# A two-trunk attention and mixture kernel: one tile of u is scaled on ScalarE before the router's exponentials instead of after them

## Chip, cores and metric

The kernel runs on one core of a Trainium2 chip. The metric is the device time of one execution in microseconds (us), lower is better. The kernel before takes 1629.51 us, the median of three executions (1629.05 to 1630.3).

## What is computed

Two independent sequences of 512 tokens with 1024 features ("trunks" 0 and 1) go through one attention layer and one expert-choice mixture of 16 experts, in float32:

```python
u = rmsnorm(h, norm_mix_g)
h = h + neighbourhood_attention(u, na_w_qkv, na_rpb, na_w_o)
u = rmsnorm(h, norm_ffn_g)
# expert_choice_ffn(u):
aff = softmax(u @ router_w, axis=-1)              # 512 x 16
gate, idx = lax.top_k(aff.T, 64)                  # each expert picks 64 tokens
xs = u[idx]
hid = silu(xs @ w_gate) * (xs @ w_up)
out = (hid @ w_down) * gate[..., None]
h = h + zeros.at[idx].add(out)
return rmsnorm(h, final_norm_g)
```

## The kernel before

Tokens lie on the 128 partitions, four tiles of 128 tokens for a trunk. The attention of trunk 0 runs first, then that of trunk 1, then a loop over the 16 experts, which handle the chosen rows of both trunks together (128 rows, 64 of each trunk). Each matrix product is made of three (high by high, high by rest, rest by high), so ScalarE casts each pair of weight rows to its high part and VectorE (DVE) subtracts to get the rest; the expert loop is a long stream of such casts, subtractions and matmuls at line 1293.

Every engine's program is written out by hand and runs in that order; the engines meet only at semaphores. The place that the change touches is the end of trunk 1's attention, where the mixture begins. There:

- TensorE (PE) makes the router's logits, `logits(b, 3)` at L1568, which count in `rt_used`. DVE computes `rstd`, one over the root mean square of h, in five small steps that end at L911 (`rstd_done`).
- DVE scales the logits and subtracts their maximum (L1186 to L1190, in `lg`). ScalarE takes the exponential in `exp_logits` (L655), and DVE turns it into affinities in `aff` (L1192 sum, L1194 reciprocal, L1196 product of `lg` and the reciprocal, both in SBUF).
- PE transposes `aff` (`turn_lists(1)`, L1501), in the middle of `early_gate_up`, matmuls of expert 0 on trunk 0's rows (L1525, L1526) that stand before and behind it in PE's order. DVE then picks the 64 best tokens of each expert in a linked chain of some forty instructions (L1112 to L1125, L1131), PE transposes the tables (`turn_tables(1)`, L1507), and DVE writes the addresses of expert 0's rows of trunk 1 in `first_rows_at` (L1145, semaphore `first_done`).
- Meanwhile ScalarE's `scale_h` (L651) multiplies each of the four tiles of h (`xh`) by its `rstd` into `arena`, and counts in `scaled`. GpSimd (POOL) waits for each, multiplies it in place by the norm's weights `grow` (L514, two inputs in SBUF), and after every second tile sends two tiles to `u_rows` in HBM (L518).
- POOL's `gather(0)` (L523) waits for all of `u_rows` and for `first_done`, and reads expert 0's 64 rows of trunk 1 back into `xh`. It has this in front of it:

```python
pool.wait_ge(u_out, 32 * TRUNKS)
pool.wait_ge(h_out, 16 * TRUNKS)
pool.wait_ge(first_done, 1)
gather(0)
```

- PE, behind `turn_tables(1)`, runs 36 transposes of the identity (L1665) whose result nobody reads, and then `first_rows` (L1620), which waits for the gathered rows. The weight loads of the next steps wait for the matmuls that follow (`pair_used`, SP's queue, L450).

ScalarE's functions come from tables; a change of table is an instruction of its own (ACT_TABLE_LOAD), and `preload_act_table` places one by hand. The copies with a scale run under any of the tables used here.

Of the kernel before, what the change touches and what calls it, by code (L numbers as in the profile page):

```python
# [21 lines left out]
ACT = mybir.ActivationFunctionType  # L22
# [19 lines left out]
TILES = T // P  # L42
# [82 lines left out]
def encoder_kernel(nc, x, g_mix, g_ffn_col, g_ffn, g_fin, w_qkv, bias, w_o, router_w, w_gate, w_up, w_down, identity, y):  # L125
# [5 lines left out]
    with ExitStack() as ctx:  # L131
# [91 lines left out]
        def bank(b, n=1):  # L223
            return ps[:, b * BANK:(b + n) * BANK]
# [332 lines left out]
        def _(act):  # L557
# [12 lines left out]
            def root(c):  # L570
                act.wait_ge(var_done, c + 2)
                cols = slice(TILES * c, TILES * (c + 1) if c < 3 * TRUNKS else TILES * c + 1)
                nc.scalar.activation(sdev[:, cols], var[:, cols], ACT.Sqrt).then_inc(sdev_done, 1)
# [31 lines left out]
            def next_high(b, g, what, last_job, q):  # L605

                wait_full(act, b, g, last_job)
                high(q, SLOT["pre" if g is None else stage_name(g)][what])

            def x_squares(b, i):  # L610

                act.wait_ge(xe_in[b][i], 16)
                if i:
                    act.wait_ge(ssq_xa, 2 * b + 1)
                square(b, early_t, i, arena[:, 0, :], ssq_xa)

            def split_x(b):
                for kc in range(KC):
                    act.wait_ge(xt_front, KC * b + kc + 1)
                    k = NORM_BANKS[kc % 4] if b else FIRST_BANKS[kc]  # L620
                    nc.scalar.activation(ut_high[:, kc * T:(kc + 1) * T], bank(k), ACT.Copy,  # L621
                                         scale=g_col[:, kc:kc + 1]).then_inc(uth_done, 1)

            def before_groups(b):
                copy_q(b, None, 0)
                copy_q(b, None, 1)
                next_high(b, None, "q", "q1", SLOTS * b + 1)

            def h_squares(b, i):

                wait_copied(act, b, GROUPS - 1, f"o{2 * i}")
                wait_copied(act, b, GROUPS - 1, f"o{2 * i + 1}")
                if i:
                    act.wait_ge(ssq_h, TILES * b + i)
                square(TRUNKS + b, xh, i, squares_junk, ssq_h)

            def copy_h(b, i):
                act.wait_ge(rt_mm, 2 * (TILES * b + i) + 1)
                nc.scalar.copy(rt[i % 2][:, 0:BANK], bank(ROUTER_BANKS[i % 2])).then_inc(rt_act, 1)

            def copy_part(b, i):
                act.wait_ge(part_mm, TILES * b + i + 1)
                nc.scalar.copy(part_lg[:, :], bank(4)[:, PART_AT:PART_AT + P]).then_inc(part_done, 1)

            def scale_h(b):

                act.wait_ge(rstd_done, b + 1)
                act.wait_ge(rt_used, TILES * (b + 1))
                for i in range(TILES):
                    at = TILES * (TRUNKS + b) + i  # L650
                    nc.scalar.activation(arena[:, i, :], xh[:, i, :], ACT.Copy, scale=rstd[:, at:at + 1]).then_inc(scaled, 1)  # L651

            def exp_logits(b):
                act.wait_ge(lg_step, 3 * (b + 1))
                nc.scalar.activation(lg[:, :, :], lg[:, :, :], ACT.Exp).then_inc(lexp_done, 1)  # L655
# [63 lines left out]
            for b in range(TRUNKS):  # L719
                group(b, 0)  # L720
                with act.Fori(1, GROUPS - 1) as g:
                    group(b, g)
                group(b, GROUPS - 1)
                if b + 1 < TRUNKS:
                    x_squares(b + 1, 0)
                    x_squares(b + 1, 2)
                copy_h(b, 0)
                if b + 1 < TRUNKS:
                    root(b + 1)
                h_squares(b, 0)  # L730
                for i in range(1, TILES - 1):
                    copy_part(b, i - 1)
                    copy_h(b, i)
                    h_squares(b, i)
                    if i == 1 and b + 1 == TRUNKS:
                        act.wait_ge(early_mm, 1)
                        nc.scalar.copy(early_xt, bank(EARLY_BANK)).then_inc(early_xt_done, 1)
                nc.scalar.preload_act_table(ACT.Sqrt)
                copy_h(b, TILES - 1)
                copy_part(b, TILES - 2)  # L740
                h_squares(b, TILES - 1)
                root(TRUNKS + b)
                copy_part(b, TILES - 1)
                if b + 1 == TRUNKS:
                    exp_logits(b)
                    scale_h(b)
                if b + 1 < TRUNKS:
                    split_x(b + 1)
                if b + 1 < TRUNKS:
                    next_high(b, GROUPS - 1, "o", "o7", SLOTS * (b + 1))  # L750
                if b + 1 < TRUNKS:
                    exp_logits(b)
                    scale_h(b)
                    before_groups(b + 1)
# [532 lines left out]
        def _(pe):  # L1287
# [322 lines left out]
            for kc in range(1, KC):  # L1610
                _, last = early_gate_up(kc)
# [135 lines left out]
```

## Time and profile before

| | |
|---|---|
| median of three executions | 1629.51 us |
| the profiled execution's own time | 1629.97 us |
| its span in the profile | 1628.2 us |
| PE busy | 98% |
| DVE busy | 78% |
| ScalarE (ACT) busy | 64% |
| POOL busy | 7% |
| chain that ended last, share on PE | 94% |

The time of an execution holds 1.77 us around the span. Attention takes the first 500 us or so, the expert loop nearly all the rest. The busy shares are averages over both; the change lies in the few microseconds in between, and there the rows in time below have to be read.

### The profile page before, as it was taken

The numbers are of one execution on the slowest core, as the hardware profiler recorded it, in microseconds if no ns is written. First come the engines' busy times: TensorE is split into PE (matmuls) and PEld (weight loads), VectorE is DVE, ScalarE is ACT, GpSimd is POOL, SyncE is SP. The second block draws the span as 40 slices with busy tenths as digits, with TensorE's granted clock in tenths as the row PEclk, the third lists the DMA queues.
The fourth block names the chain that finished last, engine by engine and source line by source line (L and its number), as shares of the span: only waits on it lengthen the run. The fifth ranks groups of instructions, "written<-read, shape, count | busy, mean of one in ns | idle before, by whom it ended". The sixth has DMA issues, their size and how long they took to land.

```text
span 1628.2 us, 22708 instructions
## 1 busy us (share of the span) xinstructions
PE 1591.7 (98%) x8288; PEld 1306.3 (80%) x8288; DVE 1264.1 (78%) x1318; ACT 1034.3 (64%) x942; POOL 110.2 (7%) x60
## 2 busy tenths in 40 slices
PE   6999999999999899999999999999999999999996
PEld 5888787888785588888888888888888888888884
DVE  6564576674565588888888888888888888888887
ACT  4443356443234577777777777777777777777774
POOL 0000002000003001001010010100101001010000
PEclk9999999999999999999999999999999999999998
DMA  9333244533243999999999999999999999999997
GB/s 362 130 109 124 74 156 176 177 113 120 78 139 124 372 405 385 387 394 367 394 391 383 397 366 395 386 384 395 367 397 384 388 396 366 393 385 388 396 349 299
DMA packets 150375, 496.15 MB, mean 305 GB/s; under 512 B 9536, under 2 KB 34240, under 8 KB 150336
## 3 DMA queue, kind: packets, MB, share of 16 engines
q1 hardware_dynamic: 140224, 459.44, 74.2%
q0 software_dynamic: 8832, 33.03, 6.4%
q10 hardware_dynamic: 1280, 3.15, 0.7%
q8 instruction: 25, 0.41, 0.1%
q14 instruction: 14, 0.11, 0.0%
HBM read 471.47 MB, written 20.97 MB: 302 GB/s over the span
## 4 chain that ended last, share of the span: by engine, by line
PE 94%; DVE 2%; DMA 2%; ACT 1%; POOL 1%; issue 0%; SPq 0%; POOLq 0%; DVEq 0%; ACTq 0%
PE ps L1293 84%; PE ps L1404 2%; PE ps L1367 2%; PE ps L1376 2%; PE ps L1661 2%; PE ps L1630 1%; DMA raw<-w_up 1%; POOL arena L514 1%; PE ps L1699 0%; DMA g_col<-g_mix 0%; DMA u_rows<-arena 0%; PE ps L1589 0%; DVE w_rest L857 0%; ACT ut_high L621 0%; PE ps L1548 0%
## 5 line engine op out<-in xcount | busy, mean ns | idle before, releaser
L857 DVE TENSOR_TENSOR w_rest<-raw,w_high 128x2048 fp32r<-128x2048 f32 x220 | 501.0, 2290 | 107.0 <-ACT w_high L795 75.3
L795 ACT CAST w_high<-raw 128x2048 fp32r<-128x2048 f32 x188 | 360.1, 1915 | 146.9 <-PE ps L1293 135.1
L1293 PE MATMUL ps<-w_high,xt_high 128*128 128x512 f32 x1000 | 311.3, 392 | 0.0
L1293 PE MATMUL ps<-w_rest,xt_high 128*128 128x512 f32 x1000 | 308.4, 390 | 0.0
L1293 PE MATMUL ps<-w_high,xt_rest 128*128 128x512 f32 x1000 | 308.3, 390 | 0.0
L857 DVE TENSOR_TENSOR w_rest<-raw_more,w_high 128x2048 fp32r<-128x2048 f32 x94 | 214.0, 2289 | 43.1 <-ACT w_high L795 43.1
L857 DVE TENSOR_TENSOR w_rest<-early,w_high 128x2048 fp32r<-128x2048 f32 x92 | 209.3, 2289 | 20.7 <-ACT w_high L795 19.3
L795 ACT CAST w_high<-raw_more 128x2048 fp32r<-128x2048 f32 x94 | 180.2, 1917 | 63.8 <-PE ps L1293 62.6
L1293 PEld LDWEIGHTS ps<-w_rest,xt_high 128*128 128x128 f32 x1000 | 188.0, 188 | 39.3
L1293 PEld LDWEIGHTS ps<-w_high,xt_rest 128*128 128x128 f32 x1000 | 188.0, 188 | 39.1
L1293 PEld LDWEIGHTS ps<-w_high,xt_high 128*128 128x128 f32 x1000 | 185.9, 188 | 36.6
L795 ACT CAST w_high<-early 128x2048 fp32r<-128x2048 f32 x92 | 176.3, 1917 | 59.8 <-PE ps L1293 59.8
L1293 PE MATMUL ps<-w_high,ht_high 128*128 128x512 f32 x496 | 154.2, 392 | 0.0
L1293 PE MATMUL ps<-w_high,ht_rest 128*128 128x512 f32 x496 | 152.8, 389 | 0.0
L1293 PE MATMUL ps<-w_rest,ht_high 128*128 128x512 f32 x496 | 152.8, 389 | 0.0
L578 ACT ACTIVATE arena<-arena,nmx 128x256 f32<-128x256 f32 x128 | 63.6, 498 | 92.9 <-DVE nmx L930 92.9
L1293 PEld LDWEIGHTS ps<-w_rest,ht_high 128*128 128x128 f32 x496 | 93.1, 188 | 19.5
L1293 PEld LDWEIGHTS ps<-w_high,ht_rest 128*128 128x128 f32 x496 | 93.1, 188 | 19.4
L1293 PEld LDWEIGHTS ps<-w_high,ht_high 128*128 128x128 f32 x496 | 91.9, 188 | 18.0
L1293 PE MATMUL ps<-ut_high,w_high 128*128 128x512 f32 x256 | 102.4, 400 | 2.5 <-DVE w_rest L857 1.3
L545 POOL DMA_INDIRECT h_rows<-xh,rows x15 | 37.6, 2504 | 965.0 <-ACT xh L784 965.0
L1293 PE MATMUL ps<-ut_rest,w_high 128*128 128x512 f32 x256 | 99.8, 390 | 0.0
(203 smaller groups left out, 2006.5 us busy)
## 6 DMA issues: line engine op xcount, KB each, us to landing
raw<-w_gate SPq DMA_DIRECT2D x64, 1024.0 KB, 7.9
raw<-w_up SPq DMA_DIRECT2D x64, 1024.0 KB, 8.5
raw<-w_down SPq DMA_DIRECT2D x64, 1024.0 KB, 7.6
raw_more<-w_gate SPq DMA_DIRECT2D x32, 1024.0 KB, 9.2
raw_more<-w_up SPq DMA_DIRECT2D x32, 1024.0 KB, 10.0
early<-w_gate SPq DMA_DIRECT2D x32, 1024.0 KB, 8.7
early<-w_up SPq DMA_DIRECT2D x32, 1024.0 KB, 9.5
raw_more<-w_down SPq DMA_DIRECT2D x32, 1024.0 KB, 8.5
```

The source lines that it names most:

```text
L514: nc.gpsimd.tensor_tensor(arena[:, i, :], arena[:, i, :], grow[:, :], ALU.mult).then_inc(xs_done, 1)
L545: pool.indirect_dma_start(h_dram, bass.IndirectOffsetOnAxis(ap=rows[:, e:e + 1], axis=0), ys, None, compute_op=ALU.add).then_inc(scattered ...
L578: nc.scalar.activation(scores[hh % 2][:, i, :], scores[hh % 2][:, i, :], ACT.Exp, bias=nmx[:, hh % 2, i:i + 1], accum_out=psum_row[:, hh % ...
L795: nc.scalar.copy(w_high[:, i % SLOTS, :], raws[i % RAW_SLOTS]).then_inc(high_done, 1)
L857: nc.vector.tensor_tensor(w_rest[:, j, :], raws[j if r is None else r], w_high[:, j, :].bitcast(F32), ALU.subtract).then_inc(rest_done, 1)
L1293: done = nc.tensor.matmul(out, lhs, rhs, start=start and part == 0, stop=stop and part == 2)
L1367: last = nc.tensor.matmul(ps[:, 6 * BANK + at:6 * BANK + at + WIN], qt[on, p, tile * P:(tile + 1) * P], kt[on, p, lo:lo + WIN], start=True ...
L1376: last = nc.tensor.transpose(ps[:, at:at + P], scores[hh % 2][:, i, c * P:(c + 1) * P], ident[:, :])
L1404: last = nc.tensor.matmul(bank(4)[a * HD:(a + 1) * HD, tile * P:(tile + 1) * P], vals, pt[:, at:at + P], start=c == 0, stop=c == 1)
L1630: last = nc.tensor.transpose(bank(6, 2)[:, kc * P:(kc + 1) * P], xg[:, kc * P:(kc + 1) * P], ident[:, :])
L1661: last = nc.tensor.transpose(bank(6, 2)[:, c * P:(c + 1) * P], hid[:, c * P:(c + 1) * P], ident[:, :])
```

## The change

For trunk 1 only, ScalarE loads the table of the exponential by itself, scales the first tile of h, takes the exponentials, and then scales the other three tiles. Before, the table load stood with the exponentials, and all four tiles behind them. Trunk 0's order stays.

```diff
-            def scale_h(b):
+            def scale_h(b, lo=0, hi=TILES):
 
                 act.wait_ge(rstd_done, b + 1)
                 act.wait_ge(rt_used, TILES * (b + 1))
-                for i in range(TILES):
+                for i in range(lo, hi):
                     at = TILES * (TRUNKS + b) + i
                     nc.scalar.activation(arena[:, i, :], xh[:, i, :], ACT.Copy, scale=rstd[:, at:at + 1]).then_inc(scaled, 1)
...
                 if b + 1 == TRUNKS:
+                    nc.scalar.preload_act_table(ACT.Exp)
+                    scale_h(b, 0, 1)
                     exp_logits(b)
-                    scale_h(b)
+                    scale_h(b, 1, TILES)
```

ScalarE's order at the end of trunk 1's attention before, with the semaphores that each instruction waits for (`gv` holds part of the logits here, L643 copies them for PE):

```order
L573 ACTIVATE sdev<-var 128x4 [waits var_done]
L643 COPY gv<-ps 128x128 [waits part_mm]
L655 ACT_TABLE_LOAD
L655 ACTIVATE lg<-lg 128x64 [waits lg_step]
L651 ACTIVATE arena<-xh,rstd 128x1024 [waits rt_used,rstd_done]
L651 ACTIVATE arena<-xh,rstd 128x1024 x3
```

And the same place of the changed kernel:

```order
L573 ACTIVATE sdev<-var 128x4 [waits var_done]
L643 COPY gv<-ps 128x128 [waits part_mm]
L745 ACT_TABLE_LOAD
L651 ACTIVATE arena<-xh,rstd 128x1024 [waits rt_used,rstd_done]
L655 ACTIVATE lg<-lg 128x64 [waits lg_step]
L651 ACTIVATE arena<-xh,rstd 128x1024 [waits rt_used,rstd_done]
L651 ACTIVATE arena<-xh,rstd 128x1024 x2
```

One scaled tile moved in front of the exponential; the table load is still one and stands where it stood. The other engines' programs are the same, line numbers apart.

## Rows read from the trace of the kernel before

**Rows 1.** The page, part 4: the chain that ended last, by line
```profile
PE ps L1293 84%; PE ps L1404 2%; PE ps L1367 2%; PE ps L1376 2%; PE ps L1661 2%; PE ps L1630 1%; DMA raw<-w_up 1%; POOL arena L514 1%; PE ps L1699 0%; DMA g_col<-g_mix 0%; DMA u_rows<-arena 0%; PE ps L1589 0%; DVE w_rest L857 0%; ACT ut_high L621 0%; PE ps L1548 0%
```

**Rows 2.** Windows: stretch, length, busy (count) of PE, PEld, DVE, ACT, POOL, PE clock, DMA
```profile
560.00:1590.00 1030.00, 1030.00 (x4728) 857.09 (x4727) 909.07 (x440) 777.77 (x455) 77.69 (x30) 1.00 1.01 386
```

**Rows 3.** The chain in order of time, 495 to 580: start, us, what
```profile
505.53 4.70 POOL arena L514 x2
...
511.29 4.70 POOL arena L514 x2
...
516.28 6.06 DMA u_rows<-arena
...
522.61 3.64 DMA xh<-u_rows,first_rows_at
...
531.29 10.17 DMA raw<-w_up
```

**Rows 4.** Timeline of ScalarE: start, us, operation [idle before <-releaser]
```profile
501.93 0.25 ACT L643 COPY gv<-ps 128x128 f32<-128x128 f32 x1
502.20 1.28 ACT L655 ACT_TABLE_LOAD   x1
504.08 0.26 ACT L655 ACTIVATE lg<-lg 128x64 f32<-128x64 f32 x1 [0.60 <-DVE lg L1190]
504.24 4.25 ACT L651 ACTIVATE arena<-xh,rstd 128x1024 f32<-128x1024 f32 x4
```

**Rows 5.** Timeline of DVE at the same place
```profile
502.87 0.16 DVE L911 TENSOR_TENSOR rstd<-newt 128x4 f32<-128x4 f32 x1
...
503.82 0.23 DVE L1190 TENSOR_TENSOR lg<-lg,lstat 128x64 f32<-128x64 f32 x1
504.37 0.22 DVE L1192 TENSOR_REDUCE lstat<-lg 128x4 f32<-128x64 f32 x1 [0.32 <-ACT lg L655]
...
504.84 0.29 DVE L1196 TENSOR_TENSOR aff<-lg,lstat 128x128 f32<-128x128 f32 x1
...
521.24 0.15 DVE L1145 SCALAR_TENSOR_TENSOR first_rows_at<-topt 64x1 uint32<-64x1 f32 x1
```

**Rows 6.** Timeline of PE at the same place
```profile
502.23 0.39 PE L1568 MATMUL ps<-adder,gv 128*128 128x16 f32 x2 [0.52 <-ACT gv L643]
...
505.19 0.63 PE L1501 MATMUL ps<-ident,aff 128*64 128x128 f32 x4 [0.69 <-DVE aff L1196]
...
519.93 0.27 PE L1507 MATMUL ps<-ident,gv 64*128 64x64 f32 x1 [1.95 <-DVE gi L1131]
...
520.20 5.82 PE L1665 MATMUL ps<-ident 128*128 128x128 f32 x36
526.29 0.70 PE L1620 MATMUL ps<-ident,xh 64*128 64x64 f32 x8 [0.28 <-DMA xh<-u_rows,first_rows_at]
```

**Rows 7.** Windows of L1665 alone: stretch, length, PE (count), PEld (count), PE clock, DMA
```profile
521.00:523.00 2.00, 2.00 (x11) 2.00 (x10) 0.50 0.78 213
524.50:525.50 1.00, 1.00 (x11) 1.00 (x10) 1.00 0.56 209
```

**Rows 8.** Timeline of POOL, the first multiply alone
```profile
505.53 2.37 POOL L514 TENSOR_TENSOR arena<-arena,grow 128x1024 f32<-128x1024 f32 x1 [4.66 <-ACT arena L651]
```

**Rows 9.** All issues of gathers at L525: ns min/median/max, first and last start
```profile
L525 POOL DMA_INDIRECT xh<-u_rows,rows x15: 990/2780/2795, 527.8 to 1506.8; - x15
```

**Rows 10.** Timeline of POOL in the expert loop
```profile
623.36 2.76 POOL L525 DMA_INDIRECT xh<-u_rows,rows  x1 [0.30 <-issue]
```

**Rows 11.** Timeline of DVE beside it
```profile
622.97 2.29 DVE L857 TENSOR_TENSOR w_rest<-raw_more,w_high 128x2048 fp32r<-128x2048 f32 x1 [1.40 <-ACT w_high L795]
```

**Rows 12.** Timeline of POOL near the end
```profile
1582.35 1.19 POOL L549 DMA_INDIRECT v<-h_rows,rows  x1 [7.87 <-DMA h_rows<-xh,rows]
```

**Rows 13.** Timeline of DVE beside it
```profile
1580.39 4.48 DVE L857 TENSOR_TENSOR w_rest<-early,w_high 128x2048 fp32r<-128x2048 f32 x2
```

## Prediction

> **What bounds the kernel now.** I read first the chain that ended last. It is matmuls of the expert loop for 84% of the span [rows 1], and from 560 to 1590 us TensorE is busy for the whole of 1030.00 us [rows 2]. Nothing in the change touches that loop. Its start is what can move: a shift of the first product of the mixture is carried to the end by an engine that never waits after it.
>
> So I read the same chain in order of time around 500 us, where attention hands over to the mixture [rows 3]. It goes through POOL's multiply of u by the norm's weights (two and two tiles, 4.70 us each pair), the second store to HBM (6.06 us, landed at 516.28 + 6.06 = 522.34), the gather of expert 0's rows (3.64 us, landed at 522.61 + 3.64 = 526.25), PE's transposes of these rows at 526.29 [rows 6], some matmuls, and a load of weights of 10.17 us that those release. POOL could begin at 505.53 because ScalarE began tile 0 at 504.24 [rows 4], 1.29 us before.
>
> Two other chains run beside it with little to spare, and the timelines show them. The list of chosen tokens: exponential, affinities, choice, and `first_rows_at` at 521.24 + 0.15 = 521.39 [rows 5], for which the gather waits too; it is 522.34 - 521.39 = 0.95 us early. And PE's own order: behind the tables' transposes at 519.93 stand 36 spare transposes that end at 520.20 + 5.82 = 526.02 [rows 6], only 0.27 us before the gathered rows are used.
>
> **The change, step by step.**
>
> *Scaling tile 0.* It needs the table (502.20 + 1.28 = 503.48), rstd (502.87 + 0.16 = 503.03) and the last logits (502.23 + 0.39 = 502.62) [rows 4 to 6]. So it begins at 503.50 in place of 504.24: 0.74 us earlier, in time in which ScalarE only waited for `lg` (0.60 us idle). POOL's first multiply, 1.29 us behind, begins at 504.79. The table load itself neither moves nor is added.
>
> *The exponential.* Four scaled tiles take 4.25 us, the last 1.13 of which is one tile by itself (an estimate from the chain's share of the first, 505.38 - 504.24), so tiles follow each other at 1.04 us. The exponential begins at 503.50 + 1.04 = 504.54 in place of 504.08: 0.46 us later. The sum at L1192, 504.37 before, moves to 504.83, and the product at L1196, 504.84 before, is due at 505.30. Tiles 1 to 3 follow from 504.70 on, in time for POOL's 2.35 us a tile.
>
> *If nothing else happened*, u would land in HBM 0.74 us earlier, at 521.60. But `first_rows_at` is then 0.46 later, at 521.85. With the 0.15 us that POOL needs from a producer's end to its start (505.38 to 505.53), the gather begins at 522.0 and lands at 525.65, 0.60 earlier. PE, however, is held 0.46 us longer at L1501, everything behind it shifts by as much, and its spare transposes end at 526.48. Their end depends on the clock: at the granted clock 0.50 some 0.21 us each, at 1.00 some 0.11 (eleven overlapping in 2.00 us and in 1.00 us) [rows 7]. At 1.00 throughout, the 36 would take about 35 x 0.11 + 0.27 = 4.1 us, 1.7 less than the 5.82 here, and end at 524.8. So the first product moves by +0.2 us (spare transposes last, the clock as in this trace) or by -0.6 us (gather last, full clock).
>
> *What POOL and DVE do to each other.* Before, DVE's last operation with both inputs in SBUF, L1196, ended at 504.84 + 0.29 = 505.13, and POOL's multiply began at 505.53: they never met [rows 5, 8]. Afterwards the multiply runs from 504.79 to 507.15 (2.37 us), and L1196 is due in the middle of it, at 505.30. The trace never shows such a pair, but it shows a related one. A gather's issue on POOL takes 990 ns at best, in the first gather, when DVE had little to do, and 2780 ns in the median, inside the expert loop [rows 9]. The one at 623.36 ended at 626.12, 0.86 us after the end (625.26) of a DVE subtraction of two SBUF inputs that had begun before it [rows 10, 11]: as though POOL had stood still until DVE was through. Against it: the gather's issue at 1582.35 took 1.19 us although DVE was in a pair of such subtractions until 1584.87 [rows 12, 13]. I take the exclusion as real and mutual, that the later one stands still until the earlier one ends. The least this costs is nothing (they overlap freely), the most the rest of the two multiplies that POOL issues back to back (to 504.79 + 4.70 = 509.49).
>
> The Trainium skill, SBUF — State Buffer, section "SBUF: two separate sides", says that a DVE operation with two SBUF inputs and a GpSimd operation that reads SBUF lock one another out for a whole instruction, whoever starts first. That speaks against this change; by it, L1196 waits for the first multiply. No row here shows DVE waiting.
>
> *Sum with the exclusion.* L1196 starts at about 507.2 in place of 504.84: 2.35 us later, and the chain of choosing with it. PE waits at L1501 with everything behind it. `first_rows_at` is ready at 521.39 + 2.35 = 523.74, past the landing of u, so the gather begins at 523.9 and lands at 527.5: +1.3 us. PE's spare transposes begin at 522.55 and end at 528.4 with the clock of this trace (+2.1) or at 526.7 at full clock. The first product is 1.3 to 2.1 us late, in the middle +1.7, all of it carried to the end. PE's longer wait at L1501 (from 0.69 to about 3 us) may cost clock on top; I bound that by the 1.7 us that it cost the spare transposes, of which matmuls that end before DVE's lists hide most.
>
> The trace is of an execution of 1629.97 us, which would become 1631.7; it lies 0.46 above the median, so for the median 1629.51 + 1.7 = **1631.2 us**. That is 0.10% and not measurable as a difference: I take 0.2%, 3.3 us, as about what this kernel's times can tell from no change.
>
> **Rivals.**
>
> *No exclusion (chance 0.36).* DVE multiplies while POOL does. Then the first product moves by -0.6 to +0.2 us and the time is 1628.9 to 1629.7. For it: the quick issue at 1582.35. Against it: fourteen slow ones.
>
> *DVE waits for both multiplies (0.08), which ends as slower.* The two are back to back (4.70 us for two of 2.37), so POOL may take the port again before DVE does. L1196 then starts at 509.5, 4.7 us late, `first_rows_at` at 526.1, the gather lands at 529.9 (+3.6) and the spare transposes end at 530.7 (+4.4): 1633.1 to 1633.9. It decides as soon as the first product is over 3.3 us late. For it: POOL leaves no gap. Against it: DVE would have asked 1.9 us before.
>
> *The change does nothing (0.02)*: were rstd or the last logits later than 504.08, tile 0 would hold up the exponential and gain nothing. Both are there by 503.03.
>
> *The clock decides (0.06).* PE's wait at L1501 lowers the clock for the matmuls behind it so that they, and not DVE's lists, end last: up to +1.7 more, 1632 to 1633.
>
> **How the numbers follow.** The forecast, exclusion for one multiply, has 0.48 and its own range 1630.6 to 1632.1 (+1.3 to +2.1, widened by the 0.5 us by which the runs before differ from their median). With no exclusion, down to 1628.7, the range is 1628.7 to 1632.4 and holds the two first cases and part of the clock's, about 0.84. Slower by over 0.2% (above 1632.8) is the wait for both and a little of the clock case: 0.09. Faster by over 0.2% (below 1626.2) needs more than the 0.74 us that POOL gains, so 0.01. The rest, 0.90, is no difference.
>
> **What would show it.** ScalarE: the table load at 502.2, a tile at 503.5, the exponential at 504.5, with no second table load. POOL: first multiply at 504.8. DVE: L1196 (two lines further down in the changed kernel) at 507.2 if the exclusion holds, with POOL's second multiply some 0.3 us later, at 505.3 if not, at 509.5 if it waits for both. POOL: the gather released by DVE's `first_rows_at`, not by u's landing, at 523.9 (or 522.0). PE: first rows' transposes at 527.5 to 528.4 (or 525.7 to 526.5), and their release by the end of the spare transposes where the clock shows 0.50 in them. I am wrong if DVE runs through POOL's multiply at its usual 0.29 us, or if the expert loop takes up the delay so that its end doesn't follow its start.

## The result, and the profile after

Over 18 executions each, the changed kernel takes 1632.13 us (median, 1630.92 to 1633.81), the kernel before 1629.62 us (1627.9 to 1631.08). The ratio is 1.0017, 95% interval 1.0011 to 1.0024: 2.5 us slower, inside the 0.2% that the prediction called no difference, but clear of noise with so many runs. It lies 0.9 us above the forecast of 1631.2, inside the range of 1628.7 to 1632.4. The times of the changed kernel lie in two groups, nine from 1630.92 to 1631.67 and nine from 1632.59 to 1633.81. The profiled execution took 1631.17 us and is of the lower group. Lines of the changed kernel behind the edit are two higher. One execution of the kernel before, in the 33 beside runs 1 to 4 below, took 1838.92 us at a granted clock of 0.821 and is left out of the ratios.

All of attention ended 1.03 us earlier in this trace than in the one before (the table load on ScalarE stands at 501.17 here, at 502.20 in [rows 4]), so I count times from that table load. The 1.03 us are not the change's: over the traces of all runs below the load starts between 501.09 and 502.20, in the changed kernel and in the kernel before alike. ScalarE's timeline (start, us, operation):

```profile
501.17 1.28 ACT L745 ACT_TABLE_LOAD   x1
502.46 1.15 ACT L651 ACTIVATE arena<-xh,rstd 128x1024 f32<-128x1024 f32 x1
503.52 0.24 ACT L655 ACTIVATE lg<-lg 128x64 f32<-128x64 f32 x1
503.66 3.21 ACT L651 ACTIVATE arena<-xh,rstd 128x1024 f32<-128x1024 f32 x3
```

The tile begins 1.29 us after the table load's start (2.04 before), the exponential 2.35 us after it (1.88 before): one is 0.75 us earlier, the other 0.47 later, and there is no second table load. POOL's timeline shows the first multiply following at once, and far down the gather:

```profile
503.76 2.35 POOL L514 TENSOR_TENSOR arena<-arena,grow 128x1024 f32<-128x1024 f32 x1 [3.92 <-ACT arena L651]
...
523.32 1.26 POOL L523 DMA_INDIRECT xh<-u_rows,first_rows_at  x1 [7.49 <-DVE first_rows_at L1147]
```

DVE's timeline is where the time went, and answers to [rows 5]:

```profile
503.79 0.22 DVE L1194 TENSOR_REDUCE lstat<-lg 128x4 f32<-128x64 f32 x1 [0.77 <-ACT lg L655]
504.04 0.18 DVE L1196 RECIPROCAL lstat<-lstat 128x4 f32<-128x4 f32 x1
504.25 2.00 DVE L1198 TENSOR_TENSOR aff<-lg,lstat 128x128 f32<-128x128 f32 x1
...
522.37 0.15 DVE L1147 SCALAR_TENSOR_TENSOR first_rows_at<-topt 64x1 uint32<-64x1 f32 x1
```

The product into `aff` shows as 2.00 us of busy time in place of 0.29. It ends at 506.25, 0.14 us after POOL's multiply ends at 503.76 + 2.35 = 506.11. The wait stands in the profile as a long instruction, not as idle time; no releaser is named. The sum and the reciprocal just before it, one input each, run at their usual 0.22 and 0.18 us inside the same multiply.

PE's timeline shows what it does behind that (compare [rows 6]):

```profile
506.31 0.62 PE L1503 MATMUL ps<-ident,aff 128*64 128x128 f32 x4 [2.85 <-DVE aff L1198]
...
521.06 0.27 PE L1509 MATMUL ps<-ident,gv 64*128 64x64 f32 x1 [1.95 <-DVE gi L1133]
...
521.33 5.82 PE L1667 MATMUL ps<-ident 128*128 128x128 f32 x36
527.48 0.71 PE L1622 MATMUL ps<-ident,xh 64*128 64x64 f32 x8 [0.34 <-DMA xh<-u_rows,first_rows_at]
```

Idle before the transposes of `aff` is 2.85 us (0.69 before). The gathered rows are used 527.48 - 501.17 = 26.31 us after the table load; before it was 526.29 - 502.20 = 24.09. That is 2.22 us later, released by the gather, which `first_rows_at` released in its turn. From the table load to the end of the span it is 1629.3 - 501.17 = 1128.13 us, before 1628.2 - 502.20 = 1126.00: the expert loop carries 2.13 us of the 2.22 to the end. The chain that ended last says it by shares: DVE has 4%, where [rows 3] had u's store and POOL's multiplies.

```profile
PE 93%; DVE 4%; DMA 1%; ACT 1%; issue 1%; POOLq 0%; ACTq 0%; SPq 0%; DVEq 0%
```

### The profile page after: what moved, and what is told of

The parts are those of the page before. It is cut to its first block, busy times and chain, and to the rows that moved or that the text cites. A ratio compares the mean times of both kernels' runs of the same rounds, so it can differ in the third digit from the quotient of the medians.

```text
span 1629.3 us, 22709 instructions
## 1 busy us (share of the span) xinstructions
PE 1591.1 (98%) x8288; PEld 1305.1 (80%) x8288; DVE 1265.4 (78%) x1318; ACT 1034.2 (63%) x942; POOL 110.3 (7%) x60
## 4 chain that ended last, share of the span: by engine, by line
PE 93%; DVE 4%; DMA 1%; ACT 1%; issue 1%; POOLq 0%; ACTq 0%; SPq 0%; DVEq 0%
PE ps L1295 83%; PE ps L1406 2%; PE ps L1369 2%; PE ps L1663 2%; PE ps L1378 2%; PE ps L1632 1%; DVE w_rest L859 1%; DMA raw<-w_up 1%; PE ps L1701 0%; DVE ut_rest L985 0%; DVE topi L1120 0%; DMA early<-x 0%; ACT arena L578 0%; DMA xh<-u_rows,first_rows_at 0%; PE ps L1550 0%
```

## Experiments

Times are medians; the ratio is to the kernel before on the same chip, with its 95% interval. "Handover" is the time from the start of ScalarE's table load to the first use of the gathered rows on PE, read from each trace as above. It is free of what happened before and after, and much sharper than the median, whose intervals are 2 to 3 us wide. Each is read from one trace; the three traces of the changed kernel have 26.18, 26.31 and 26.33, and run 5, with the same work as the kernel before, has 24.06 against its 24.09.

| | median (n), us | before (n), us | ratio [95%] | product into aff, us | handover, us |
|---|---|---|---|---|---|
| before | | 1629.62 (18) | | 0.29 | 24.09 |
| changed | 1632.13 (18) | 1629.62 (18) | 1.0017 [1.0011, 1.0024] | 2.00 | 26.31 |
| 1 POOL waits for aff | 1629.95 (11) | 1629.42 (33) | 1.0004 [0.9995, 1.0013] | 0.29 | 24.41 |
| 2 reciprocal in PSUM | 1629.98 (11) | 1629.42 (33) | 1.0004 [0.9995, 1.0013] | 0.29 | 24.43 |
| 3 before, reciprocal in PSUM | 1629.98 (11) | 1629.42 (33) | 1.0003 [0.9994, 1.0012] | 0.29 | 24.20 |
| 4 as 2, 30 spare transposes | 1630.87 (11) | 1629.42 (33) | 1.0012 [1.0003, 1.0021] | 0.29 | 24.42 |
| 5 before, explicit table load | 1629.93 (10) | 1629.76 (25) | 0.9999 [0.9989, 1.0008] | 0.29 | 24.06 |
| 6 before, extra op, two inputs | 1631.07 (10) | 1629.76 (25) | 1.0011 [1.0001, 1.0020] | 0.29 | 25.58 |
| 7 before, extra op, one input | 1631.03 (10) | 1629.76 (25) | 1.0008 [0.9999, 1.0018] | 0.29 | 25.69 |
| 8 changed, PE kept busy | 1631.93 (11) | 1629.78 (15) | 1.0013 [1.0004, 1.0022] | 2.03 | 26.24 |
| 9a, 9b changed again | 1630.71, 1632.89 (1 each) | 1629.78 (15) | | 2.01, 2.00 | 26.18, 26.33 |
| 10 changed, POOL in quarters | 1630.93 (11) | 1629.51 (15) | 1.0008 [0.9999, 1.0017] | 0.37 | 24.54 |

**1. POOL waits for the affinities.** The collision is taken away and ScalarE's new order is kept.

```diff
                     pool.wait_ge(scaled, TILES * b + i + 1)
+                    if b + 1 == TRUNKS and i == 0:
+                        pool.wait_ge(aff_done, 3 * (b + 1))
```

> The changed kernel, but POOL's first multiply of trunk 1 also waits for the affinities (aff_done), so it can't run beside DVE's product of two SBUF inputs. Exclusion theory: the product takes 0.29 us again (2.00 in the changed kernel), POOL's multiply begins about 0.45 us after the product's start, the list of tokens is late by the exponential's 0.46 us alone and u lands about when it did before; the time is 1629.6 to 1630.1, some 2 to 2.5 us under the changed kernel. Rival (the order on ScalarE itself costs the time, through the later exponential or the clock): the time stays at 1631.5 to 1632.5.

1629.95 us, as the exclusion says. The timelines of DVE and of POOL in this run:

```profile
505.20 0.29 DVE L1200 TENSOR_TENSOR aff<-lg,lstat 128x128 f32<-128x128 f32 x1
```
```profile
505.67 4.71 POOL L516 TENSOR_TENSOR arena<-arena,grow 128x1024 f32<-128x1024 f32 x2 [4.89 <-DVE aff L1200]
```

The handover falls from 26.31 to 24.41 us. What is left over the kernel before is 0.32 us. The later exponential accounts for it: `first_rows_at` ends 521.75 - 502.11 = 19.64 us after the table load, 0.45 later than before.

**2 and 3. The same product with one SBUF input.** POOL still starts early; DVE's second operand moves to a free part of PSUM bank 4. Run 2 puts this on the changed kernel, run 3 on the kernel before.

```diff
-                nc.vector.reciprocal(lstat[:, b, 2, :], lstat[:, b, 1, :]).then_inc(aff_done, 1)
+                inv = lstat[:, b, 2, :] if b + 1 < TRUNKS else bank(4)[:, 2 * P:2 * P + TILES]
+                nc.vector.reciprocal(inv, lstat[:, b, 1, :]).then_inc(aff_done, 1)
...
-                                        lstat[:, b, 2, :].rearrange("p (i a n) -> p i a n", a=1, n=1).broadcast_to([P, TILES, 2, E]),
+                                        inv.rearrange("p (i a n) -> p i a n", a=1, n=1).broadcast_to([P, TILES, 2, E]),
```

> The changed kernel, but for trunk 1 the reciprocal that multiplies lg lies in PSUM, so that the product into aff has one SBUF input in place of two; POOL starts early and nobody waits more. Exclusion by two SBUF inputs: the product takes about 0.29 us though POOL's multiply runs, the first product of gathered rows is -0.6 to +0.2 us against before, the time 1629.0 to 1629.8. Rival (POOL's multiply holds up any DVE operation that starts beside it, or the two together use up a shared bandwidth): the product still takes about 2 us and the time stays at 1631.5 to 1632.5.

> The kernel before with the reciprocal of trunk 1 in PSUM: the control for the run above. Every theory expects no change, 1629.2 to 1630.0, with the product at 0.25 to 0.35 us.

The timelines of DVE and POOL of run 2:

```profile
505.12 0.29 DVE L1199 TENSOR_TENSOR aff<-lg,ps 128x128 f32<-128x128 f32 x1
```
```profile
504.61 4.69 POOL L514 TENSOR_TENSOR arena<-arena,grow 128x1024 f32<-128x1024 f32 x2 [3.92 <-ACT arena L651]
...
522.53 1.26 POOL L523 DMA_INDIRECT xh<-u_rows,first_rows_at  x1 [5.86 <-DVE first_rows_at L1147]
```

The product now runs in the middle of POOL's multiply and takes 0.29 us: not POOL's activity as such, but the second SBUF operand makes this product wait. Yet with the collision gone and POOL 0.74 us early, the kernel gains nothing: handover 24.43 us. The gather is released by the list of tokens, which is 0.5 us late (521.73 - 502.02 = 19.71 against 19.19), nearly all of it the exponential's 0.47. The handover is 0.34 us over before, and so a little above the expected -0.6 to +0.2. So what the change is good for at best is hidden by its own other half. The medians of runs 2 and 3 are both 0.56 us over before with intervals that hold 1; the control is as far off as the edit, so this difference means nothing.

**4. Fewer spare transposes on top of run 2.**

```diff
-            for _ in range(36):
+            for _ in range(30):
```

> The changed kernel with the reciprocal in PSUM and 30 spare transposes in place of 36. If the spare transposes hold up the gathered rows there, the rows are used as soon as they land, 0.6 us earlier than before, and the time is 1629.0. If fewer transposes let the clock stay or fall low for the matmuls behind them, up to 1.7 us are lost again: 1630 to 1631.5.

1630.87 us and slower (1.0012), with a handover of 24.42 us like run 2. The spare transposes did not hold up the rows in run 2's trace (the gather did), so there was nothing to gain. The loss must lie behind the handover; the profiled execution, 1629.63 us, was the quickest of the eleven and doesn't show it. The clock may be the cause (below); that is not shown.

**5. One part of the change alone: the explicit table load, nothing moved.**

```diff
                 if b + 1 == TRUNKS:
+                    nc.scalar.preload_act_table(ACT.Exp)
                     exp_logits(b)
                     scale_h(b)
```

> The kernel before with the exponential's table loaded by an instruction of its own and nothing moved: one part of the change alone. Every theory that blames the moved tile expects 1629.2 to 1630.0 and the same instructions on ScalarE. Were the explicit load the cost, 1.3 us more.

No change (0.9999), handover 24.06 us. The load costs nothing; it replaces the one that stood there.

**6 and 7. The collision by itself, in the kernel before.** One small DVE operation is put between the two copies that fill trunk 1's lists, while POOL multiplies. Its result is read by nobody.

```diff
                 for h in range(2):
...
+                    if b + 1 == TRUNKS and h == 0:
+                        # run 6:
+                        nc.vector.tensor_tensor(newt[:, 2, 0:TILES], newt[:, 0, 0:TILES], newt[:, 1, 0:TILES], ALU.mult)
+                        # run 7 instead:
+                        nc.vector.tensor_scalar(newt[:, 2, 0:TILES], newt[:, 0, 0:TILES], 1.0, None, ALU.mult)
```

> The kernel before with one extra DVE operation on 128x4 elements with two SBUF inputs, between the two copies that fill trunk 1's lists, while POOL's first multiply runs. Exclusion theory: it waits for the end of the multiply, takes 1.3 to 1.7 us in place of about 0.2, and the lists are late by as much; the time is 1.0 to 1.7 us above before. Rival (no exclusion for such operations, the 2 us of the product had another cause): it takes 0.2 us, and the time is as before.

> The same place with an extra operation on 128x4 elements with one SBUF input. Exclusion by two SBUF inputs: 0.2 us, and the time is as before within 0.3 us. If any DVE operation is held up, it takes as long as the one with two inputs.

DVE's timeline of run 6, then of run 7, each with POOL's first multiply behind it:

```profile
505.88 1.56 DVE L1115 TENSOR_TENSOR newt<-newt 128x4 f32<-128x4 f32 x1
```
```profile
505.04 2.38 POOL L514 TENSOR_TENSOR arena<-arena,grow 128x1024 f32<-128x1024 f32 x1 [4.66 <-ACT arena L651]
```
```profile
505.80 1.57 DVE L1115 TENSOR_SCALAR newt<-newt 128x4 f32<-128x4 f32 x1
```
```profile
504.97 2.38 POOL L514 TENSOR_TENSOR arena<-arena,grow 128x1024 f32<-128x1024 f32 x1 [4.67 <-ACT arena L651]
```

Four elements per partition with two inputs take 1.56 us in place of 0.16 (the same kind of operation at L904 of the kernel before, when POOL is idle) and end at 507.44, with POOL's multiply at 505.04 + 2.38 = 507.42. The handover is 25.58 us, 1.49 over before, the median 1.3 us. That is a piece of the change's cost with nothing of the change in it. Run 7 refutes my expectation: an operation with one input and a constant waits just as long (ends at 507.37, POOL at 507.35). So "two SBUF inputs" is too narrow a rule. Beside POOL's multiplies a reduction (0.22 us) and a reciprocal (0.18 us) in the changed kernel, and copies from PSUM (0.41 to 0.42 us) and MAX8 (0.42 us) in runs 6 and 7, were not held. The Trainium skill, SBUF — State Buffer, section "SBUF: two separate sides", has a second clause that would take in run 7, DVE operations in a two-port performance mode; that fits, but no run here shows which mode an instruction is in.

**8 and 9. The two groups of times.** Run 8 is the changed kernel with PE kept busy while it waits for `aff`; 9a and 9b are the changed kernel unchanged.

```diff
             early_gate_up(0)
+            for _ in range(24):
+                nc.tensor.transpose(bank(EARLY_BANK)[:, 0:P], ident[:, :], ident[:, :])
             turn_lists(1)
```

> The changed kernel, but PE makes 24 transposes of the identity (about 2.6 us) in its longer wait for the affinities, ahead of the transposes of aff. The changed kernel's times lie in two groups, nine near 1631.4 and nine near 1633.2. If the clock lost to that wait is what makes the upper group, it empties and the median is 1631.0 to 1631.6. If the upper group comes from another place (the spare transposes, or the wait for the gathered rows) or isn't the clock, some 4 or 5 of 11 runs stay near 1633.2 and the median is 1631.4 to 1633.2.

> The changed kernel once more, for a trace of its upper group if the run falls in it. If the clock makes the group, a run near 1633.2 shows a granted clock of 0.50 for longer, or at a place where PE has more to do, than the trace of 1631.17 us; if not, its clock is the same and another wait is longer by 1.8 us.

> As the run before it: the changed kernel once more, for a trace of its upper group.

9a (1630.71 us) fell in the lower group, 9b (1632.89) in the upper. Windows of PE in 9a, then in 9b (stretch, length, busy (count), granted clock, DMA share, GB/s):

```profile
507.00:510.50 3.50, 3.50 (x12) 0.54 0.01 6
521.50:525.50 4.00, 4.00 (x36) 1.00 0.02 4
...
528.00:531.50 3.50, 3.29 (x22) 1.00 0.24 23
```
```profile
507.00:510.50 3.50, 3.50 (x10) 0.56 0.11 46
521.50:525.50 4.00, 4.00 (x36) 1.00 0.10 16
...
528.00:531.50 3.50, 3.46 (x12) 0.53 0.24 29
```

In both the clock is at 1.2 GHz for a while from about 507 us, after PE's 2.85 us of waiting for `aff`, and it costs nothing there: PE reaches `turn_tables` with 0.29 and 0.26 us of idle left. In both the spare transposes run at 2.4 GHz, and end 1.9 and 2.0 us before the gathered rows are used; the handover is 26.2 to 26.3 us all the same, so it is the gather that sets it. But in 9b alone the clock is low from 528, in the first matmuls on the gathered rows, after some 2 us in which PE waited for the gather (9a waited 1.87 us and kept its clock). Those matmuls release the next loads of weights, which the chain in order of time shows (9a, then 9b):

```profile
532.77 9.72 DMA raw<-w_up
548.14 1.94 PE ps L1663 x8
```
```profile
533.94 9.53 DMA raw<-w_up
549.13 1.94 PE ps L1663 x8
```

From the gathered rows' first use to that load it is 532.77 - 527.76 = 5.01 us in 9a and 533.94 - 527.54 = 6.40 in 9b, 1.4 more; by the transposes at L1663 it is 1.2 (20.38 and 21.59 us). That is about half of what separates the two executions, 1631.1 - 1628.9 = 2.2 us of span. The rest comes right behind L1663, in the first products of the expert loop, where the clock is low too. Windows of PE some 2 us after the start of L1663, in 9a, then in 9b:

```profile
550.00:556.00 6.00, 6.00 (x25) 0.86 1.03 423
```
```profile
551.00:557.00 6.00, 6.00 (x19) 0.65 1.02 416
```

In both PE waited over 5 us for `xh` before L1663, and in 9b the clock stays low for longer behind it. From L1663 to the end it is 1080.76 us in 9a and 1081.97 in 9b, another 1.2 us. (9b's table load came 0.37 us earlier and its handover is 0.15 longer, which makes up the sum.) So in this pair of traces the clock makes the difference, at two places.

The second place is not the changed kernel's own. Over all 13 traces the stretch from those transposes to the end lasts 1080.76 to 1081.97 us, and is shorter the higher the granted clock of its first 8 us (0.78 down to 0.62): it spreads the times of every kernel here by up to 1.2 us. The first place shows in two traces of 13: 9b, and that of run 3 (1632.02 us), with the product at 0.29 us, a handover of 24.20 and a granted clock of 0.80 over 528 to 540 us. So it needs neither the moved tile nor the collision. In the five traces whose spare transposes ran at full clock (runs 3, 5, 9a, 9b, 10) PE then waited 1.87 to 2.04 us for the gather, and in two of them the clock was low behind that wait; in the other eight the clock was low in the spare transposes, PE waited at most 0.81 us, and the clock was at 1.00 behind.

Whether the nine times of the changed kernel's upper group come from the same place is not shown, since none of them has a trace; only 9b has one. The kernel before has no such group among its 18 times beside the changed kernel's (none is more than 1.5 us above the median), though beside runs 8 and 9 three of its 15 times lie 1.6 to 1.8 above. Why the changed kernel has more of them stays open. Run 8 speaks against PE's wait for `aff` as what costs the time: that wait was filled, the handover stayed at 26.24 us and the median at 1631.93, 2.15 over before. The expectation had 4 or 5 of 11 times near 1633.2 if that wait was not the cause, and none if it was. One lies in the upper group, but six lie between the two groups and four in the lower, so I read nothing into that.

**10. POOL's first tile in four instructions.**

```diff
-                    nc.gpsimd.tensor_tensor(arena[:, i, :], arena[:, i, :], grow[:, :], ALU.mult).then_inc(xs_done, 1)
+                    parts = 4 if b + 1 == TRUNKS and i == 0 else 1
+                    for s in range(parts):
+                        cols = slice(s * D // parts, (s + 1) * D // parts)
+                        nc.gpsimd.tensor_tensor(arena[:, i, cols], arena[:, i, cols], grow[:, cols], ALU.mult).then_inc(xs_done, 1)
                     if i % 2:
-                        pool.wait_ge(xs_done, TILES * b + i + 1)
+                        pool.wait_ge(xs_done, TILES * b + i + 1 + (3 if b + 1 == TRUNKS else 0))
```

> The changed kernel, but POOL multiplies tile 0 of trunk 1 in four instructions of a quarter each (about 0.6 us), the other tiles whole. If DVE waits for the end of POOL's running instruction and takes its turn before the next, the product into aff, due 0.5 us after POOL's start, lasts 0.3 to 0.9 us in place of 2.00, the lists are late by 0.5 to 1.1 us and the time is 1630.0 to 1630.8. If POOL's next instruction, already in its queue, goes first each time, the product still lasts 2 us or more (or until the last of the tile's or all five instructions) and the time is 1631.4 to 1633.

DVE's timeline, and POOL's first quarter:

```profile
504.72 0.37 DVE L1201 TENSOR_TENSOR aff<-lg,lstat 128x128 f32<-128x128 f32 x1
```
```profile
504.22 0.72 POOL L517 TENSOR_TENSOR arena<-arena,grow 128x256 f32<-128x256 f32 x1 [3.92 <-ACT arena L654]
```

The product ends at 505.09, 0.15 us after the first quarter's end at 504.94. DVE waits for POOL's running instruction only, and gets its turn though three more quarters are queued. How it gets in is not shown: POOL's records have the second quarter follow the first without a gap (1.46 us for both), and spans on POOL are rough. The handover is 24.54 us, 1.77 under the changed kernel. The median, 1630.93 (1.0008 [0.9999, 1.0017]), is 1.4 above before, just over the expected 1630.0 to 1630.8 and more than the handover's 0.45 says; its interval holds both.

## Why the prediction was right

**The mechanism.** DVE's product of two SBUF operands was held by POOL's multiply until that ended. The trace after shows it, runs 1, 2 and 10 each take it away in another way and the handover returns to within 0.45 us of before, and run 6 makes it in the kernel before. The related rows that the prediction leaned on (the issue of gathers, [rows 9 to 11]) pointed the right way, and the counterexample [rows 12, 13] was none for this pair. The rule of the Trainium skill that the prediction names agrees with the trace: 2.00 us in place of 0.29. "Mutual" is not shown. The prediction had POOL's second multiply start some 0.3 us late, behind DVE's product; the two multiplies take 4.71 us together against 4.69 before.

**The step on ScalarE.** Tile 0 earlier by 0.74 (measured 0.75), the exponential later by 0.46 (measured 0.47), no added load: right.

**The size of the wait.** The list of tokens was to be 2.35 us late. `first_rows_at` ends at 522.52 in the changed kernel, 21.35 us after the table load, against 521.39 - 502.20 = 19.19 before: 2.16 late. I had added a fresh 0.29 us of work behind POOL's end, where 0.14 is seen.

**The handover, +1.7 in the middle, was mis-sized.** It was +2.22, just above the 1.3 to 2.1 that the sum allowed. The term that was too small is POOL's step from `first_rows_at` to the gather. I took 0.15 us from a wait for ScalarE in front of a plain multiply; here it is 523.32 - 522.52 = 0.80, the same 0.80 in runs 1 and 2. The gather is also longer, 4.12 us from its start to landing against 3.64. So the chain through the gather came to 522.52 - 501.17 + 0.80 + 4.12 = 26.27 us after the table load, 2.22 later than before (526.25 - 502.20 = 24.05), where I had 1.3. The spare transposes came out nearly as predicted: they end at 521.33 + 5.82 = 527.15, 2.16 later than before, for the 2.35 that I had (the list was less late by as much). The gather and not they was last, by 0.3 us. That the measured 2.22 lies so near the upper end of the sum is luck, since that end was worked out for the other chain, PE's own.

Most of the gather's extra length is no cost of the change. It is the trace before that is the odd one: its issue of the gather takes 0.93 us there and 1.26 in the twelve other traces, among them those of runs 3 and 5 without the change. In those twelve a subtraction of two SBUF operands on DVE (L1237 in the changed kernel, 0.69 us) starts 0.23 to 0.24 us before the issue; before, it ended just as the issue began. That looks like the exclusion in the other direction, but no run tests it.

**The rivals.** No exclusion is refuted. A wait for both multiplies is refuted by the trace, where the product ends 0.14 us after the first. The clock rival has a part that I placed wrongly: after PE's wait for `aff` the clock does fall in 9a and 9b, but that is hidden; in 9b it costs 1.2 us on the first matmuls of the gathered rows and as much again at the start of the expert loop. The median moved by 2.5 us, and not by the 1.7 of the forecast, partly by the handover's 0.5 us more and partly by the upper group; the shares are not shown. The 1632.13 us lie in the clock rival's 1632 to 1633, and just outside the forecast's own 1630.6 to 1632.1, so the median alone would not tell the two apart: the traces do, since all three of the changed kernel have the late handover and only one the low clock behind it.

**The gain that was never there.** Even free of the collision (run 2) the early tile gains nothing. In the trace before I had u's landing last, by 0.95 us. But counted with POOL's 0.80 us, the list allowed the gather at 522.19 at the earliest, 0.4 us before it started at 522.61. That trace also had a slow store: 6.06 us against 5.2 in runs 3 and 5. In run 5's trace u landed at 515.24 + 5.19 = 520.43, and the gather started only at 521.14, 0.80 us after `first_rows_at` ended at 520.34, although the profile names the store as its releaser. So there the list was last, and the two are near a tie: the change delays the one that is usually last to hasten the other.

## What to carry to other kernels

Before starting GpSimd's elementwise work earlier, list the small DVE operations that will then fall inside it: one of 0.29 us can take the rest of a 2.35 us instruction, and shows as a long instruction, not as a wait. An operand in PSUM, GpSimd's work cut in short instructions, or a wait that keeps the two apart each took the wait away here, though none of them made this kernel faster than before. And where two chains meet in one gather, find which is last with the waiting engine's own start-up counted in, before trading time between them.

## What was not expected of the hardware

- A DVE operation with a single SBUF input and a constant, on 128x4 elements, was held for 1.57 us by GpSimd's multiply, as long as one with two inputs (1.56 us), while a reduction (0.22 us), a reciprocal (0.18 us) and a product with its second operand in PSUM (0.29 us) were not.
- GpSimd started an indirect DMA 0.80 us after the DVE operation that released it, but a multiply 0.15 us after ScalarE's.
